# Feed-forward bodies with the next chunk's weights split earlier, both down projections last, and the activations' sums moved from GpSimd

## The reference

```python
def swiglu(h, w_gate, w_up, w_down):
    return (jax.nn.silu(h @ w_gate) * (h @ w_up)) @ w_down
...
    for l in range(DEPTH):
        x = x + 0.5 * swiglu(rms_norm(x, ffn1_norm[l]), ffn1_w_gate[l], ffn1_w_up[l], ffn1_w_down[l])
        h = rms_norm(x, mix_norm[l])
        z = h @ w_in[l]
...
        a = neighborhood_attention(q, k, v, rpb[l])
        m = multiscale_pool(p, w_pool[l], pool_scale[l])
        x = x + jnp.concatenate([a, m], axis=-1) @ w_out[l]
        x = x + 0.5 * swiglu(rms_norm(x, ffn2_norm[l]), ffn2_w_gate[l], ffn2_w_up[l], ffn2_w_down[l])
    return rms_norm(x, final_norm)
```

## Time and profile before

| | |
|---|---|
| median of 3 runs | 935.62 us |
| the runs | 934.34 to 936.62 us |
| profiled execution | 933.16 us |
| its span | 931.4 us |
| TensorE busy | 913.9 us, 98% |
| VectorE busy | 702.2 us, 75% |
| ScalarE busy | 540.1 us, 58% |
| GpSimd busy | 116.5 us, 13% |

### The profile page before, as it was taken

How to read it: one execution, slowest core, us unless ns; L and a number is a source line. 1 busy time by engine, 2 the same in 40 slices (tenths; PEclk the granted TensorE clock), 3 DMA queues, 4 the chain that set the end, 5 groups by cost and what they waited for, 6 DMA issues and landing times.

```text
span 931.4 us, 12711 instructions
## 1 busy us (share of the span) xinstructions
PE 913.9 (98%) x4217; PEld 738.7 (79%) x4217; DVE 702.2 (75%) x898; ACT 540.1 (58%) x793; POOL 116.5 (13%) x124
## 2 busy tenths in 40 slices
PE   8999999999999999999999999999999999999997
PEld 6787877887778887887888878878877878778786
DVE  5999398468766998598379986874687479968854
ACT  6775365456647666365376655553775486546543
POOL 2310110110003311110033101000100033001000
PEclk9999999999999999999999999999999999999999
DMA  7868977975234968978558568658434277666641
GB/s 249 306 135 235 222 170 230 267 250 202 90 124 159 314 117 236 259 190 210 145 187 310 115 217 284 197 179 304 131 143 139 88 269 218 211 225 161 225 158 46
DMA packets 132412, 184.30 MB, mean 198 GB/s; under 512 B 8672, under 2 KB 108176, under 8 KB 132112
## 3 DMA queue, kind: packets, MB, share of 16 engines
q1 hardware_dynamic: 117744, 165.43, 52.0%
q0 software_dynamic: 11296, 14.77, 11.8%
q10 hardware_dynamic: 3328, 3.54, 1.1%
HBM read 182.58 MB, written 4.19 MB: 201 GB/s over the span
## 4 chain that ended last, share of the span: by engine, by line
PE 65%; DVE 8%; ACT 5%; issue 4%; DMA 4%; POOL 1%; DVEq 0%; SPq 0%; ACTq 0%; POOLq 0%
PE ps L1382 19%; PE ps L1385 19%; PE ps L1383 18%; DMA w_raw<-in_ffn_w_down_dram 4%; DVE w_lo_f L1009 2%; DVE w_raw L1123 2%; DVE w_lo L1009 1%; PE ps L1491 1%; PE ps L1443 1%; PE ps L1392 1%; PE ps L1393 1%; PE ps L1465 1%; PE ps L1679 1%; ACT w_hi L655 1%; ACT w_hi_f L671 1%
## 5 line engine op out<-in xcount | busy, mean ns | idle before, releaser
L1009 DVE TENSOR_TENSOR w_lo<-w_raw,w_hi 128x1024 fp32r<-128x1024 f32 x200 | 250.0, 1295 | 81.7 <-ACT w_hi L655 81.6
L655 ACT ACTIVATE w_hi<-w_raw 128x1024 fp32r<-128x1024 f32 x184 | 183.0, 1050 | 82.6 <-PE ps L1385 49.2
L1382 PE MATMUL ps<-w_hi,gt_hi 128*128 128x512 f32 (+1 forms) x356 | 140.1, 394 | 3.0 <-DVE w_lo L1009 1.7
L1383 PE MATMUL ps<-w_lo,gt_hi 128*128 128x512 f32 (+1 forms) x356 | 137.9, 387 | 0.0
L1382 PE MATMUL ps<-w_hi,xs_hi 128*128 128x512 f32 x288 | 114.0, 396 | 0.0
L1382 PE MATMUL ps<-w_hi,xt_hi 128*128 128x512 f32 x272 | 110.8, 407 | 2.6 <-DVE w_lo L1020 2.1
L1385 PE MATMUL ps<-w_hi,xs_lo 128*128 128x512 f32 x288 | 112.4, 390 | 0.0
L1383 PE MATMUL ps<-w_lo,xs_hi 128*128 128x512 f32 x288 | 112.2, 390 | 0.0
L1385 PE MATMUL ps<-w_hi,gt_lo 128*128 128x512 f32 (+1 forms) x356 | 109.9, 387 | 0.0
L1020 DVE SCALAR_TENSOR_TENSOR w_lo<-w_raw,gains,w_hi 128x512 fp32r<-128x512 f32 x128 | 94.1, 791 | 19.3 <-ACT w_hi L662 16.1
L1383 PE MATMUL ps<-w_lo,xt_hi 128*128 128x512 f32 x272 | 106.2, 391 | 0.0
(11 more groups left out here) (146 smaller groups left out, 1524.8 us busy)
## 6 DMA issues: line engine op xcount, KB each, us to landing
w_raw<-in_ffn_w_down_dram SPq DMA_DIRECT2D x88, 512.0 KB, 6.5
w_raw<-in_ffn_w_gate_dram SPq DMA_DIRECT2D x54, 512.0 KB, 4.1
w_raw<-in_ffn_w_up_dram SPq DMA_DIRECT2D x54, 512.0 KB, 5.2
w_raw<-in_w_in_dram SPq DMA_DIRECT2D x32, 512.0 KB, 5.3
w_raw_e<-in_ffn_w_gate_dram SPq DMA_DIRECT2D x16, 512.0 KB, 4.9
w_raw_e<-in_ffn_w_up_dram SPq DMA_DIRECT2D x16, 512.0 KB, 6.6
w_raw_f<-in_ffn_w_gate_dram SPq DMA_DIRECT2D x16, 512.0 KB, 6.3
w_raw_f<-in_ffn_w_up_dram SPq DMA_DIRECT2D x16, 512.0 KB, 7.2
```

Source lines behind the costliest of these rows:

```text
L655: nc.scalar.activation(w_hi[slot][:, part], w_raw[raw][:, part], ACT.Copy).then_inc(hi_ready[slot], 2)
L1009: nc.vector.tensor_tensor(w_lo[slot][:, part], w_raw[raw][:, part], w_hi[slot][:, part].bitcast(F32), ALU.subtract).then_inc(lo_ready[slot ...
L1382: nc.tensor.matmul(o, hi, wh, start=start, stop=False)
L1383: nc.tensor.matmul(o, hi, wl, start=False, stop=False)
```

## The change

It rearranges the feed-forward bodies on all engines, moves the activations' sums to other engines, and builds the bias table in another way.

**Slots and loads.** In a body, raw tile b is filled with the next ordinary chunk's first unit once the second weight sum has been formed, and raw tile e with a down unit once the third has. The sums are formed in e instead of b. In the diffs a new line takes the place of the removed ones near it.

```diff
-                    free(e, 3 * j)
+                    n = pair_no(layer, ff, j)
+                    free(d, 3 * j + 1)
                     load_gate_up(layer, weights, i + 2, 0, e)
-                    free(d, 3 * j + 1)
-                    free(a, 4 * j + 2)
+                    free(b, 3 * j + 2)
                     load_down(layer, weights, i - 1, d)
                     free(f, 3 * j)
                     load_gate_up(layer, weights, i + 1, 0, f)
-                    free(a, 4 * j + 3)
+                    free(a, 3 * j + 3)
                     load_gate_up(layer, weights, i + 2, 1, a)
-                    free(b, 2 * j + 3)
+                    free(b, 3 * j + 3)
                     load_gate_up(layer, weights, i + 1, 1, b)
                     free(d, 3 * j + 2)
                     load_down(layer, weights, i, d)
-                    free(e, 3 * j + 2)
-                    load_gate_up(layer, weights, i + 3, 0, e)
+                    sp.wait_ge(sum_ready, 3 * n + 2)
+                    load_gate_up(layer, weights, i + 3, 0, b)
                     free(f, 3 * j + 2)
                     load_gate_up(layer, weights, i + 3, 1, f)
                     free(d, 3 * j + 3)
                     load_down(layer, weights, i + 1, d)
-
-                    sp.wait_ge(sum_ready, 3 * pair_no(layer, ff, j) + 3)
-                    load_down(layer, weights, i + 2, b)
-                    free(a, 4 * j + 5)
+                    sp.wait_ge(sum_ready, 3 * n + 3)
+                    load_down(layer, weights, i + 2, e)
+                    free(a, 3 * j + 5)
                     load_gate_up(layer, weights, i + 4, 0, a)
-                    free(d, 3 * j + 4)
+                    free(e, 3 * j + 3)
                     load_gate_up(layer, weights, i + 4, 1, b)
-                free(a, 4 * BODIES + 2)
+                free(b, 3 * BODIES + 2)
                 load_down(layer, weights, LAST - 1, d)
-                free(a, 4 * BODIES + 3)
+                free(a, 3 * BODIES + 3)
                 load_down(layer, weights, LAST, a)
```

```diff
                 sum_hi(a, a, (sum_ready, 3 * n + 3), (m_ready, 7 * n + 3))
+                plain(e, b, 3 * j + 4, (m_ready, 7 * n + 5))
                 act.wait_ge(combined, 7 * n + 4)
                 silu_pair(p1, 0, 1)
-                plain(e, e, 2 * j + 1, (m_ready, 7 * n + 5))
+                plain(f, f, 2 * j + 1, (m_ready, 7 * n + 6))
                 act.wait_ge(combined, 7 * n + 6)
                 silu_pair(m5, 1, 0)
-                plain(f, f, 2 * j + 1, (m_ready, 7 * n + 6))
+                plain(b, d, 3 * j + 3, (m_ready, 7 * n + 4))
                 act.wait_ge(combined, 7 * n + 7)
                 silu_pair(u, 1, 1)
-                store_gt_hi(layer, ff, i + 1)
-                plain(a, d, 3 * j + 3, (m_ready, 7 * n + 7))
-                plain(d, b, 3 * j + 4, (down_used, down_no(layer, ff, i + 2)))
+                plain(d, e, 2 * j + 1, (down_used, down_no(layer, ff, i + 2)))
+                store_gt_hi(layer, ff, i + 1, 1)
                 silu_of(layer, ff, 2 * j + 3, 0)
                 store_gt_hi(layer, ff, i + 2)
-                plain(a, a, 2 * j + 4, (down_used, down_no(layer, ff, i + 3)))
-                plain(b, b, 3 * j + 5, (m_ready, 7 * n + 4))
+                plain(a, a, 2 * j + 4, (m_ready, 7 * n + 7))
                 silu_of(layer, ff, 2 * j + 3, 1)
+                plain(b, b, 3 * j + 5, (down_used, down_no(layer, ff, i + 3)))
```

```diff
+                dve.wait_ge(lo_ready[f], 4 * unit_no(layer, ff["stage"], f, 3 * j) + 5)
+                add_units(e, b)
...
-                lo(e, 3 * j + 1, b)
+                lo(e, 3 * j + 1, e)
...
-                add_units(a, b)
+                dve.wait_ge(lo_ready[a], 4 * unit_no(layer, ff["stage"], a, 3 * j + 3) + 5)
+                add_units(a, e)
...
                 gate_pair(p1, gated_x, 0, 1, 4 * n + 2)
+                lo(e, 3 * j + 2, b)
                 dve.wait_ge(m_ready, 7 * n + 6)
                 combine(u, ps[:, BANK_Y, :], u, ALU.add)
                 combine(m5, ps[:, BANK_Y, :], m5, ALU.subtract)
-                lo(e, 3 * j + 2, e)
+                lo(f, 3 * j + 2, f)
+                gate_pair(m5, gated_x, 1, 0, 4 * n + 3)
                 dve.wait_ge(m_ready, 7 * n + 7)
                 dve.wait_ge(combined, 7 * n + 5)
                 combine(u, ps[:, BANK_X, :], u, ALU.subtract)
-                gate_pair(m5, gated_x, 1, 0, 4 * n + 3)
-                lo(f, 3 * j + 2, f)
+                lo(b, 3 * j + 4, d)
                 gate_pair(u, gated, 1, 1, 4 * n + 4)
-                store_gt_lo(layer, ff, i + 1)
-                lo(a, 4 * j + 5, d)
-                lo(d, 3 * j + 3, b)
+                store_gt_lo(layer, ff, i + 1, 1)
+                lo(d, 3 * j + 3, e)
                 store_gt_lo(layer, ff, i + 2)
                 gate(layer, ff, 2 * j + 3, 0)
-                lo(a, 4 * j + 6, a)
-                lo(b, 2 * j + 4, b)
+                lo(a, 3 * j + 5, a)
                 gate(layer, ff, 2 * j + 3, 1)
+                lo(b, 3 * j + 5, b)

             def ff_stage(layer, ff, following=None):
```

```diff
-                whole_down(layer, ff, i + 1, a, 4 * j + 5)
-                pe.wait_ge(pair_gated, 4 * n + 4)
-                transpose_tiles(gated)
+                ordinary(layer, ff, 2 * j + 3, 0, (e, f), units)
+                pe.wait_ge(pair_gated, 4 * n + 3)
+                transpose_tiles(gated_x)
+
+                def transpose_y():
+                    pe.wait_ge(pair_gated, 4 * n + 4)
+                    pe.wait_ge(gt_lo_ready, gt_no(layer, ff, i + 1) + 1)
+                    transpose_tiles(gated)
+
                 pe.wait_ge(combined, 7 * n + 6)
-                ordinary(layer, ff, 2 * j + 3, 1, (e, f), units)
+                ordinary(layer, ff, 2 * j + 3, 1, (e, f), units, {4: transpose_y})
+                whole_down(layer, ff, i + 1, b, 3 * j + 4, buf=1)
                 whole_down(layer, ff, i + 2, d, 3 * j + 3)
```

```diff
+            def scale_x(layer, ff, ks):
+
...
+                act.wait_ge(xt_hi_ready, number * 4 + 4)
...
+                for k in ks:
+                    nc.scalar.activation(normed[:, :, k * P:(k + 1) * P],
+                                         xt_hi[:, :, k, :].bitcast(F32), ACT.Copy,
                                          scale=gains[:, ff["stage"], layer, k:k + 1]
                                          ).then_inc(x_scaled, 1)
...
-                act.wait_ge(x_scaled, KT * (n + 1))
+                act.wait_ge(x_summed, KT * (n + 1))
...
+            def add_low_x(layer, ff, ks):
...
+                dve.wait_ge(xt_lo_ready, number * 4 + 4)
+                for k in ks:
+                    dve.wait_ge(x_scaled, KT * n + k + 1)
+                    part = normed[:, :, k * P:(k + 1) * P]
+                    nc.vector.scalar_tensor_tensor(
+                        part, xt_lo[:, :, k, :].bitcast(F32), gains[:, ff["stage"], layer, k:k + 1],
+                        part, ALU.mult, ALU.add).then_inc(x_summed, 1)
...
+            def sum_blocks(layer, ff):
...
+                dve.wait_ge(x_lo_ready, 4 * n + 2)
+                nc.vector.tensor_tensor(block(1, 1), block(1, 1), block(1, 0), ALU.subtract
+                                        ).then_inc(s_summed, 1)
+                dve.wait_ge(s_summed, 4 * n + 1)
+                nc.vector.tensor_tensor(block(1, 0), block(0, 0), block(1, 0), ALU.add
+                                        ).then_inc(s_summed, 1)
```

```diff
+                scale_x(layer, ff, range(4, KT))
                 split_hi(d, d, raw_no(layer, stage, d, 0), (down_used, down_no(layer, ff, 1)))
-                scale_x(layer, ff)
+                x_hi(layer, ff)
                 store_gt_hi(layer, ff, 0)
-                x_hi(layer, ff)
                 silu_of(layer, ff, 1, 0)
+                s_hi(layer, ff)
                 split_hi(a, a, raw_no(layer, stage, a, 2), (g0_used, ord_no(layer, ff, 1) + 1))
                 silu_of(layer, ff, 1, 1)
                 split_hi(b, b, raw_no(layer, stage, b, 2))
-                s_hi(layer, ff)
```

```diff
+                first = layer * N_HEADS * rpb_head + (WIN_ROWS - 4) * RPB_ROW + WIN_COLS - 1
+                for half in range(2):
+                    src = bass.AP(rpb.tensor, first + 4 * half * rpb_head,
+                                  [[rpb_head, 4], [-1, GRID_W], [1, SPAN + RPB_ROW]])
+                    pool.dma_start(bias_dram[layer, 4 * half:4 * half + 4, :, :], src
+                                   ).then_inc(bias_rows_loaded, 16)
...
+                for half in range(2):
+                    for rq in range(P // GRID_W):
+                        shift = (1 - rq) * RPB_ROW
+                        src = bias_dram[layer, 4 * half:4 * half + 4, :, shift:shift + SPAN]
+                        dst = spans(half)[rq * GRID_W:(rq + 1) * GRID_W, :]
+                        pool.dma_start(dst.rearrange("p (h s) -> p h s", h=4),
```

(19 more changed lines are left out.)

133 lines of the change are left out of this document (48 added, 85 removed).

## The result

| | before | after |
|---|---|---|
| median of 4 runs | 935.03 us | 921.50 us |
| the runs | 934.34 to 936.62 | 921.39 to 922.14 |
| profiled execution | 933.16 | 921.39 |
| its span | 931.4 | 919.6 |

The ratio is 0.9855, 95% interval 0.9841 to 0.987: 13.5 us faster, where 6.0 had been forecast. A second thing to see is the spread: 2.3 us before, 0.75 after.

The account below looks back on a forecast made before the run. It bounded the gain at 13.9 us, TensorE's priced stops. Removing 13.9 (10.7 + 3.2) and adding 7.9 (2.0 + 3.3 + 2.6) took 933.16 to 927.2; with the median's 2.46 offset 929.6, range 923.5 to 935.0.

Parts of the forecast that it names:

- The ceiling and the price of a stop: TensorE's stops: each costs its idle time plus 0.16 us; in all 13.9 us, the most that can be gained.
- The stops that remain in first bodies: Unit f in four first bodies: 0.3 us late, about 0.5 each with its price, 2.0 us in all.
- Second bodies without a stop: Second bodies: e's low part fills VectorE's 2.02 us hole, f is ready 2.3 us sooner, no stop left.
- the inner transposes without a price: Bodies: transposes waiting for the chunk before's low part, written 550.7, wanted 550.9; 0.2 us of room, no charge.
- the down unit on time: Bodies: earlier refills and fewer bias transfers bring the down unit's load on time, removing the 1.4 us gt_lo stop.
- The openings: Stage openings: 3.2 us of stops go; s_hi delays unit a of chunk 2, 3.3 us new in three stages.
- The first stage: First opening: TensorE gains 2.4 us at the start, then pays 2.6 us new through late units.
- The bias table: Four transfers replace 32; the mixing stage is charged nothing, and the late down unit's stop goes.
- Rival 1: Openings: the sums are not late, 3 to 5 of 5.9 us come back; 921.7 to 926.5, chance 0.22.
- Rivals 2 to 4: Bodies give back gains (934 to 936.5, 0.12); chained sums slow openings (939, 0.1); down unit late (932 to 933.5, 0.06).
- rival 4: Bodies: earlier loads do not bring the down unit on time; 932 to 933.5, chance 0.06.
- The stretched splits: Openings: VectorE's splits, 4.39 us for two beside GpSimd's sums against 2.35, would lose the stretching whole.

Follow-up runs that it names:

- unit_a_first: The changed kernel with ScalarE's split of unit a for the third chunk put ahead of s_hi; 914.40 us.
- body_bias: The changed kernel with the activations' sums back on GpSimd; 920.41 us.
- body_sums: The changed kernel with the old bias table (32 gathers, one load of 1.5 MB); 928.10 us.
- body_only: The kernel before with only the bodies' new order and loads, activations' sums and bias table as before; 923.56 us.
- sums_only: The kernel before with only the activations' sums moved off GpSimd; 939.17 us.
- blocks_pool: unit_a_first with the four chained block sums back on GpSimd; 931.65 us.
- bias_only: The kernel before with only the bias table's new transfers; 931.39 us.
- gathers_long: The kernel before with its 32 table transfers reading 1536-byte rows of a weight matrix instead of 256-byte runs, giving wrong biases; 931.48 us.

## Why the prediction failed

From one profiled execution to the other it forecast -6.0 and -11.8 was measured; carrying the old median's offset over added another 2.3 of error. By its own steps:

- **The ceiling and the price of a stop: the step that failed most.** "In all 13.9 us, and no more than that can be gained" priced a stop at its idle time plus 0.16 before it. unit_a_first, in which no wait of TensorE after the first 16 us is longer than 0.12, is 18.9 us shorter in span. The bodies alone held 530.33 - 515.92 = 14.4 us where it had 10.7. An undisturbed second body has two stops with 0.53 us idle ((2.5 + 1.7)/8) and costs 1.17 more than one without: 0.32 a stop beyond its idle time, twice the 0.16. The other half is behind the stop: the next matmul starts 0.11 late (the next transpose 0.05), the ones after it by hundredths, and unit e's second matmul is 0.07 late in that body without any idle time. Missed: 3.7 us.
- **The stops that remain in first bodies.** Forecast 2.0, measured 1.55 (517.47 - 515.92), of which 0.7 is the tail of the opening's stop. The walk's place was right, unit f and nothing else. Its lateness, 0.3, was 0.05 to 0.1. With the openings of before (body_bias) it is 0.16 to 0.28 in three first bodies, at most 0.12 of it idle, and with what lies behind it 0.3 to 0.4, below the 0.5 forecast. That the opening's own stop gave VectorE the difference in the changed kernel is not shown: unit_a_first has neither stop.
- **Second bodies without a stop, the inner transposes without a price, the down unit on time**: right. The reason for the last was half wrong: the order of the loads was not enough while the gathers were there (body_sums, 3.74 us).
- **The openings.** A stop of 0.93 idle in three stages, 1.1 of price: measured 1.19 idle and 1.34 to 1.35 at the front. The mechanism, s_hi ahead of unit a's split, is confirmed by unit_a_first. The first stage was forecast to lose 0.2 on balance (2.6 new for 2.4 removed), and won 0.97: against unit_a_first, 2.55 went and 1.58 came. Its units of chunk 1 were walked too late, since TensorE does not stop for them at all; the stop at the third chunk is there, 1.35 idle against 1.7. The other three were forecast to lose 2.5 (3.3 new for 0.8 removed) and lost 2.09. That this is near is luck: 3.99 came (355.89 - 351.90) and 1.90 went (353.80 - 351.90), both more than forecast. Together 1.6 missed.
- **The bias table.** "Nothing is charged", and 1.5 us for the one stop seen. By the ratios it is worth 4 to 5 us a run in the old kernel; by medians it is 3.2 with the new bodies alone (body_only to body_bias) and 6.6 in the changed kernel (body_sums). The sum was made against one execution in which that stop was short, and the 2.46 us by which the median lay above it was carried over as a constant. It went with the gathers: the changed kernel's median lies 0.1 above its profiled execution. Missed: 2.35.
- **Rivals.** Rival 1 (the openings' term mostly not there) was the nearest, at 921.7 to 926.5; what happened is nearly its time, by other causes: the openings' term was there. Rivals 2 to 4 did not occur in the changed kernel. What body_sums shows in a first body is rival 4's late down unit, by another cause.
- **The stretched splits.** They fell back to 1218 ns: two halves took 4.39 beside GpSimd's sums and 2.35 or 2.36 in every opening after. The Trainium skill's page SBUF — State Buffer, section Who interferes with whom, says that a VectorE instruction with two SBUF inputs contends with a GpSimd instruction that reads SBUF; the two traces agree with that. But the stretching had cost little, since body_bias keeps it and is the faster kernel of the two.
- **The clock.** "At its upper level in every slice" held for the trace that was read and for the one after. It did not hold for every kernel: behind some stops of 1.75 us and more the clock fell, and no price of a stop in the prediction has that in it.

What stays open: why the clock falls behind one stop and not behind another of the same length, how much of the old kernel's spread is gathers and how much the clock behind them (its seven quickest runs, 932.8 to 933.6, have a mean granted clock of 0.998 to 1.000, its three slowest, over 940, 0.994 to 0.996), and how much of f's lateness the opening's stop hid.

## To carry to other kernels

Price a stop against a stretch of the same instructions without one, not by its idle time: here short stops of 0.2 to 0.35 us idle cost about 0.3 more than that. A stop of 1.75 us or more may cost another 1.7 to 2.5 us at the lower clock, so look at the pitch of the matmuls behind it. When the runs of a kernel spread and its profiled execution is at their low end, look for a transfer of many small pieces beside the loads before carrying the difference over as a constant. And when an engine stands waiting with ready work queued behind, swap the two first: that one line was worth 7.1 us, more than the 6.0 that had been forecast for the whole change.

## What the runs showed of the hardware

Two 512 KB loads issued among transfers of 96 KB in pieces of 256 bytes landed after 11.4 and 18.6 us (15.0 in the middle) in the slowest of twelve executions, against 8.1 without those transfers. Executions of the kernel with thirty-two such transfers lay between 932.8 and 942.7 us; with as many and as large transfers in pieces of 1536 bytes between 930.2 and 932.1, as with four larger transfers in their place (930.7 to 931.8).

A float32 matmul of 128x512 that had to wait started 0.16 us later than its idle time explains, and was followed by one that started 0.11 us late by itself. After a wait before a set of four transposes the second of them was 0.05 late.

TensorE's granted clock fell to 0.50 (1.2 GHz) within some matmuls behind stops of 6.07 us (sums_only), 3.74 (body_sums), one of four of 2.65 to 2.81 (blocks_pool) and some of 1.75 at the start (bias_only, gathers_long, but not before, body_only or body_bias). Matmuls then started 0.43 us apart instead of 0.23, for six to eleven matmuls, which cost 1.7 to 2.5 us. Behind stops of 1.5 us and less no trace shows it past the first 5 us of the program.
